# Late modulation on VectorE, query tiles inside the expert stage, and one stage for the even layer's gating and compression

## The reference

```python
mod = silu(c) @ ada_w + ada_b
shift1, scale1, gate1, shift2, scale2, gate2 = jnp.split(mod, 6, axis=-1)
h = rms_norm(x, norm1_g) * (1.0 + scale1) + shift1
z = h @ w_in
att = dilated_mixture_attention(qa, ka, va); rw = rwkv7_bidirectional(...)
x = x + gate1 * (concat([att, rw]) @ w_out)
h2 = rms_norm(x, norm2_g) * (1.0 + scale2) + shift2
q = h2 @ w_query                       # 8 heads of 2 x 128
s1, s2 = q[..., :half] @ sub_keys1.T, q[..., half:] @ sub_keys2.T
# top 16 of each, top 16 of their 256 sums: 16 of 16384 experts per head
ff = sum over 128 experts of gate * gelu(h2 . u_e) * v_e
x = x + gate2 * ff
```

## Time and profile before

| | us |
|---|---|
| median of 3 executions | 2421.84 |
| the profiled execution | 2421.19 |
| its span | 2418.1 |
| TensorE / VectorE / ScalarE / GpSimd busy | 2016.3 / 1547.4 / 1012.2 / 458.9 |
| opening | 0 to 39.5 |
| input projection | 39.5 to 118.6 |
| shift, attention, feature stage | 118.6 to 198.4 |
| recurrence features | 198.4 to 291.9 |
| query projection, scoring | 478.2 to 549.2 |
| experts | 549.2 to 1216.3 |
| swiglu, then norm | 1216.3 to 1428.6 |
| even projection, gating, compression | 1428.6 to 1550.3 |
| last norm, store | 2401.1 to 2418.1 |

### The profile page before, as it was taken

How to read it: one execution, slowest core, us unless ns; L and a number is a source line. 1 busy time by engine, 2 the same in 40 slices (tenths; PEclk the granted TensorE clock), 3 DMA queues, 4 the chain that set the end, 5 groups by cost and what they waited for, 6 DMA issues and landing times. The chain is left out here.

```text
span 2418.1 us, 33750 instructions
## 1 busy us (share of the span) xinstructions
PE 2016.3 (83%) x12086; PEld 1510.8 (62%) x12086; DVE 1547.4 (64%) x2670; ACT 1012.2 (42%) x2036; POOL 458.9 (19%) x475
## 2 busy tenths in 40 slices
PE   4988899695777777778789977899998998648997
PEld 4867888572222232222279976657997987437996
DVE  6577244657767667666456655366676776776665
ACT  3433011333444344444355544156665554315553
POOL 0010023004444443444200000001121433320000
PEclk9965599888999999999999988599999999769999
DMA  7533300237999999999845533114554554204552
GB/s 289 171 100 103 119 3 3 87 124 304 420 419 420 420 420 420 419 420 418 365 139 184 190 123 130 41 39 142 187 191 148 189 181 158 83 35 149 190 184 84
DMA packets 104092, 496.57 MB, mean 205 GB/s; under 512 B 11792, under 2 KB 17040, under 8 KB 71088
## 3 DMA queue, kind: packets, MB, share of 16 engines
q1 hardware_dynamic: 65376, 224.42, 27.8%
q0 software_dynamic: 36864, 268.45, 26.8%
q10 hardware_dynamic: 1744, 2.29, 0.3%
HBM read 494.07 MB, written 1.05 MB: 205 GB/s over the span
## 5 line engine op out<-in xcount | busy, mean ns | idle before, releaser
L239 PE MATMUL ps<-srcs,wh 128*128 128x512 f32 x2064 | 746.8, 403 | 49.1 <-DVE srcs L253 31.0
L1602 PE MATMUL ps<-row,diag 128*128 128x512 f32 x1024 | 507.4, 626 | 155.8 <-ACT diag L1641 155.7
L241 PE MATMUL ps<-srcs,wl 128*128 128x256 f32 x2064 | 586.5, 284 | 0.0
L221 DVE TENSOR_TENSOR wl<-ring,wh 128x1024 fp32r<-128x1024 f32 x362 | 450.2, 1248 | 130.2 <-ACT wh L215 128.6
L239 PEld LDWEIGHTS ps<-srcs,wh 128*128 128x128 f32 x2064 | 395.6, 192 | 144.7 <-issue 40.6
L1602 PEld LDWEIGHTS ps<-row,diag 128*128 128x128 f32 x1024 | 180.0, 193 | 481.8 <-ACT diag L1641 338.5
L1722 DVE CUSTOM_DVE_ANT_0 row<-row,h_tok 128x1024 f32<-128x1024 f32 x256 | 313.7, 1225 | 210.9 <-DMA row<-in_peer_uv,experts 209.1
L215 ACT ACTIVATE wh<-ring 128x1024 fp32r<-128x1024 f32 x362 | 379.5, 1052 | 120.7 <-DMA ring<-in_stream 56.1
L241 PEld LDWEIGHTS ps<-srcs,wl 128*128 128x128 f32 x2064 | 398.9, 193 | 0.1
L1585 POOL DMA_INDIRECT row<-in_peer_uv,experts x256 | 267.4, 1045 | 375.9 <-PE ps L1602 354.4
L231 PE MATMUL ps<-hidh,wh 128*128 128x256 f32 x704 | 199.3, 283 | 9.0 <-DVE hidl L716 6.2
(11 more groups left out here) (449 smaller groups left out, 2319.7 us busy)
## 6 DMA issues: line engine op xcount, KB each, us to landing
ring<-in_stream SPq DMA_DIRECT2D x410, 512.0 KB, 3.3
row<-in_peer_uv,experts POOLq DMA_INDIRECT x256, 15.4
bias<-in_attn_bias SPq DMA_DIRECT2D x8, 256.0 KB, 4.1
w<-in_cmp_w SPq DMA_DIRECT2D x1, 2048.0 KB, 7.2
xT<-in_xT ACTq DMA_DIRECT2D x1, 1024.0 KB, 25.5
out_xT<-hT SPq DMA_DIRECT2D x1, 1024.0 KB, 4.4
lora<-in_lora_up SPq DMA_DIRECT2D x1, 512.0 KB, 3.8
ws<-in_gm_w SPq DMA_DIRECT2D x1, 512.0 KB, 3.4
```

Source lines behind the costliest of these rows:

```text
L221: nc.vector.tensor_tensor(wl[:, n % PAIRS, :], ring[:, tile % RING, :], wh[:, n % PAIRS, :].bitcast(F32), ALU.subtract).then_inc(tiles_fre ...
L239: nc.tensor.matmul(out, wh[:, n, cols], source.rearrange("p a t -> p (a t)"), start=start, stop=stop, skip_group_check=True)
L241: return nc.tensor.matmul(out[:, 0:S], wl[:, n, cols], source[:, 0, :], start=False, stop=stop, skip_group_check=True)
L1602: last = nc.tensor.matmul(y_part(t, half), diag[:, s % DIAGS, :], row[:, s % ROWS, D + half * 512:D + (half + 1) * 512], start=(slot == 0) ...
```

## The change

- The opening loads `xT` on SP's queue behind the first six tiles, takes the mean square ahead of the first column on TensorE, and scales it between two of the last sums on VectorE.
- The 32 late modulation tiles leave the stream. SP loads them from `ada_late` into six slots that lie in `alpha`, `beta`, `kappa`; VectorE adds them up (`late_add`), 20 in the input projection, one per tile, and 12 in the feature stage; TensorE makes 32 columns of the four sums (`late_column`) in the places of the old products. Per stage there is one addition to `mod`. The input projection now also prepares the next projection's first two tiles.
- The query projection and the scoring move into the expert stage: four heads' tiles (8) at its start, interleaved with the choice of heads 0 and 1, the other 8 tiles among the first four heads' slots. Scores are copied by ScalarE instead of VectorE.
- Two swiglus compute the squares and `rstd` at their end; the norm's product goes into the even projection and into the last stage, which stores in four parts from two queues.
- Gating and compression are one stage; its 12 tables are loaded during the projection, ahead of its refills on SP; the compression matmuls alternate between the two halves.

The core of the diff (indentation cut by eight, lines that only move left out):

```diff
     def _(sp):
         for i in range(RING):
             sp.dma_start(ring[:, i, :], A["stream"][i]).then_inc(loaded[i], 16)
+        sp.dma_start(xT[:, :, :], A["xT"].rearrange("(k p) t -> p k t", p=P)).then_inc(x_in, 16)
-        act.dma_start(xT[:, :, :], A["xT"].rearrange("(k p) t -> p k t", p=P)).then_inc(x_in, 16)
...
         dve.wait_ge(c_ready, 1)
         for i in range(T_ADA):
             total, k, slot = acc[:, i // KT, :], i % KT, i % RING
+            if i == T_ADA - 3:
+                dve.wait_ge(summed, 1)
+                nc.vector.tensor_scalar(rstd[:, :], ps[:, 7, 0:S], 1.0 / D, NORM_EPS, ALU.mult, ALU.add
+                                        ).then_inc(scaled, 1)
...
-        take_rstd(dve, summed, scaled, root, inverted)
-        for n in range(AHEAD):
-            low(dve, T_ADA + n)
+        dve.wait_ge(root, 1)
+        nc.vector.reciprocal(rstd[:, :], rstd[:, :]).then_inc(inverted, 1)
+        low(dve, T_ADA)
         dve.wait_ge(columns, 1)
         nc.vector.tensor_tensor(mod[:, 0:T_ADA], ps[:, 0, 0:T_ADA], vec_all("ada_b")[:, 0:T_ADA], ALU.add
                                 ).then_inc(v, 1)
         dve.wait_ge(v, 1)
         nc.vector.scalar_tensor_tensor(gs[:, 0, :], mod[:, 8:16], 1.0, vec_all("norm1_g"), ALU.add, ALU.mult)
+        low(dve, T_ADA + 1)
...
         pe.wait_ge(mats_in, 16)
+        mean_square(pe, squared, summed)
         column(0)
-        mean_square(pe, squared, summed)
         column(1).then_inc(columns, 1)
-def late_load(sp, chunk, count=1):
-    refill(sp, LATE + (chunk - 2) * KT, count * KT)
-def late_tile(pe, chunk, k, begins, counted=None):
-    tile = LATE + (chunk - 2) * KT + k
-    pe.wait_ge(loaded[tile % RING], 16 * (tile // RING + 1))
+late_in = [sem(f"late_in{i}") for i in range(LATE_RING)]
+late_used = sem("late_used")
+def late_load(sp, i):
+    if i >= LATE_RING:
+        sp.wait_ge(late_used, i - LATE_RING + 1)
+    sp.dma_start(late_slot(i), A["ada_late"][i]).then_inc(late_in[i % LATE_RING], 16)
+def late_add(dve, i):
+    k, slot = i % KT, i % LATE_RING
+    total = late_sum(i // KT)
+    dve.wait_ge(late_in[slot], 16 * (i // LATE_RING + 1))
+    if k == 0:
+        last = nc.vector.tensor_scalar(total, late_slot(i), cs[:, k:k + 1], None, ALU.mult)
+    else:
+        dve.wait_ge(late_used, i)
+        last = nc.vector.scalar_tensor_tensor(total, late_slot(i), cs[:, k:k + 1], total, ALU.mult,
+                                              ALU.add)
+    last.then_inc(late_used, 1)
+def late_column(pe, u):
+    pe.wait_ge(late_used, KT * (u + 1))
     for j in range(KT):
+        last = nc.tensor.matmul(ps[:, 7, u * KT + j:u * KT + j + 1], late_sum(u)[:, j * P:(j + 1) * P],
+                                mat("ones")[:, 0:1], start=True, stop=True)
+    return last
...
         @block.sync
         def _(sp):
-            refill(sp, first, total)
+            if loads:
+                loads(sp)
+            if late_count:
+                for i in range(total):
+                    refill(sp, first + i, 1)
+                    if i < late_count:
+                        late_load(sp, i)
+            else:
+                refill(sp, first, total)
...
             for i in range(tok_count):
                 low(dve, first + AHEAD + i)
+                if i < late_count:
+                    late_add(dve, i)
...
-        norm=(lambda k: gs[:, 0, k:k + 1], lambda k: mod[:, k:k + 1]), ahead=False)
-take(T_ADA_LATE)
+        norm=(lambda k: gs[:, 0, k:k + 1], lambda k: mod[:, k:k + 1]), late_count=LATE_W_IN)
...
             nc.tensor.matmul(ps[:, b, :], mat("blockones"),
                              sq[:, 2 * b:2 * b + 2, :].rearrange("p a t -> p (a t)"),
                              start=True, stop=True).then_inc(summed, 1)
-        for k in range(KT):
-            late_tile(pe, 2, k, k == 0)
+        late_column(pe, 0)
+        late_column(pe, 1).then_inc(late_summed, 1)
...
-        late_mod(dve, 2)
+        dve.wait_ge(late_summed, 1)
+        nc.vector.tensor_tensor(mod[:, 16:32], ps[:, 7, 0:16], vec_all("ada_b")[:, 16:32], ALU.add)
...
     def _(sp):
         sp.dma_start(lora[:, :, :], A["lora_up"]).then_inc(ups_in, 16)
         sp.dma_start(g_up[:, :], A["g_up"]).then_inc(ups_in, 16)
+        for i in range(LATE_W_IN + LATE_RING, ADA_LATE):
+            late_load(sp, i)
...
         nc.vector.tensor_tensor(sq[:, 0:4, :], kk[:, :, :], kk[:, :, :], ALU.mult)
+        for i in range(LATE_W_IN, ADA_LATE):
+            late_add(dve, i)
...
-    def _(sp):
-        late_load(sp, 3, 3)
...
-        for chunk in (3, 4, 5):
-            for k in range(KT):
-                late_tile(pe, chunk, k, chunk == 3 and k == 0)
+        late_column(pe, 2)
+        late_column(pe, 3).then_inc(late_summed, 1)
         pe.wait_ge(kb_ready, 1)
...
-        for n in range(AHEAD):
-            high(act, LATE + T_ADA_LATE + n)
...
-        late_mod(dve, 3, 3).then_inc(mod_in, 1)
+        dve.wait_ge(late_summed, 1)
+        nc.vector.tensor_tensor(mod[:, 32:48], ps[:, 7, 16:32], vec_all("ada_b")[:, 32:48], ALU.add
+                                ).then_inc(mod_in, 1)
         dve.wait_ge(mod_in, 1)
         nc.vector.scalar_tensor_tensor(gs[:, 1, :], mod[:, 32:40], 1.0, vec_all("norm2_g"), ALU.add, ALU.mult)
-        for n in range(AHEAD):
-            low(dve, LATE + T_ADA_LATE + n)
...
+        def query(i):
+            pe.wait_ge(tiles_freed, first + i + 1)
+            if i >= 2:
+                pe.wait_ge(query_out, i - 1)
+            for k in range(KT):
+                if i == 0:
+                    pe.wait_ge(src_low, k + 1)
+                last = product_both(query_bank(i), first + i, k, srcs[:, k], k == 0, k == KT - 1)
+            last.then_inc(tiles_used, 1)
...
+        def score(h):
+            pe.wait_ge(query_out, 2 * h + 2)
+            for t in range(TT):
+                for half in range(2):
+                    last = nc.tensor.matmul(score_bank(h)[:, (2 * t + half) * NE:(2 * t + half + 1) * NE],
+                                            queries[:, (2 * h + half) % 4, t * P:(t + 1) * P],
+                                            subkeys[:, half, :], start=True, stop=True)
+            last.then_inc(scored, 1)
...
+        query(0)
+        query(1)
+        pe.wait_ge(keys_in, 16)
+        score(0)
+        turn_h()
+        for h in range(1, EARLY):
+            query(2 * h)
+            query(2 * h + 1)
+            if h >= 2:
+                score(h - 1)
+        score(EARLY - 1)
...
             last.then_inc(v_used, 1)
+            ahead = s // TOPK + EARLY
+            if ahead < NH:
+                if s % TOPK == 3:
+                    query(2 * ahead)
+                if s % TOPK == 8:
+                    query(2 * ahead + 1)
+                if s % TOPK == 13:
+                    score(ahead)
...
+        def copy_low(i):
+            act.wait_ge(tiles_used, split_no(first + i) + 1)
+            nc.scalar.activation(low_part[:, i % 2, :], query_bank(i)[:, S:2 * S], ACT.Copy
+                                 ).then_inc(low_copied, 1)
...
+        for k in range(KT):
+            act.wait_ge(normed, k + 1)
+            nc.scalar.activation(srch[:, k, :], hT[:, k, :], ACT.Copy).then_inc(src_high, 1)
+        weight_and_copy(0)
+        weight_and_copy(1)
+        copy_scores(0)
+        for t in range(TT):
+            act.wait_ge(h_turned, t + 1)
+            nc.scalar.activation(h_tok[:, t, :], ps[:, 2 * t:2 * t + 2, :].rearrange("p b n -> p (b n)"),
+                                 ACT.Copy).then_inc(h_copied, 1)
+        for h in range(1, EARLY):
+            weight_and_copy(2 * h)
+            weight_and_copy(2 * h + 1)
+            if h >= 2:
+                copy_scores(h - 1)
+        copy_scores(EARLY - 1)
...
+            ahead = s // TOPK + EARLY
+            if ahead < NH:
+                if s % TOPK == 5:
+                    weight_and_copy(2 * ahead)
+                if s % TOPK == 10:
+                    weight_and_copy(2 * ahead + 1)
+                if s % TOPK == 15:
+                    copy_scores(ahead)
...
+            if head < NH:
+                dve.wait_ge(score_copied, 2 * head + 2)
...
+        def weight(i):
+            low(dve, first + AHEAD + i)
+        def out(i):
+            dve.wait_ge(low_copied, i + 1)
+            if i >= 4:
+                dve.wait_ge(scored, i // 2 - 1)
+            nc.vector.tensor_tensor(queries[:, i % 4, :], query_bank(i)[:, 0:S], low_part[:, i % 2, :], ALU.add
+                                    ).then_inc(query_out, 1)
...
+        weight(0)
+        out(0)
+        weight(1)
+        out(1)
+        def early_tile():
+            if early() % 4 == 0:
+                at = early.now // 4 + 3
+                if at < 4 * EARLY:
+                    (out if at % 2 else weight)(at // 2)
         for head in range(LOOKAHEAD):
-            choose(head, lambda: None)
+            choose(head, early_tile)
...
+                ahead = head + EARLY
```

(44 more changed lines are left out.)

396 lines of the change are left out of this document (203 added, 193 removed).

## The result

The change takes the median from 2419.5 us (2412.9 to 2422.5, 4 runs) to **2301.4 us** (2296.9 to 2304.4, 4 runs): ratio 0.951, 95% interval 0.949 to 0.954. The profiled execution took 2296.9 us, its span 2295.1 instead of 2418.1, 123.0 us less.

A forecast was written before the change was run, and what follows sets the result against it. The prediction took no engine to bound the whole kernel, each stretch having its own limit. Its terms summed to -121.5 us from the profiled 2421.2, giving 2300 us, with a range of 2285 to 2319.

The forecast's parts named there:

- rival of late tiles: Input projection: late tiles landing in 6.6 us set the pace, 20 steps +9.5, feature stage +2, 2311 us in all; 12%.
- Opening, -1.5: Opening: x lands sooner and the mean square is taken earlier, so the modulation ends at 37.8 us; 1.5 us less.
- Recurrence features, -45: Recurrence's features: the 42.76 us wait behind TensorE's narrow records and two low parts (2.35) go; stage 47 to 49 us.
- features, +3.2: Feature stage: twelve late sums on VectorE take 15.7 us where it idled 12.48; the end moves from 198.3 to 201.5.
- Query projection and scoring, -34.9: Expert stage: gathers start 47 us earlier, less 11.2 for ring loads among them and 0.9 for late row recycling.
- The rival of gathers held up by TensorE in the first four heads: Expert stage: TensorE falls behind in the first four heads, at half clock for 25 us; +13, 2313 us; 8%.
- The rival of a choice that waits: Expert stage: head 0's experts come only after all eight early query tiles; +9, 2309 us; 4%.
- Gating and compression, -36.4: Gating and compression: two stages become one, the 9.7 us table wait goes, paired records take 13.2 instead of 26.3 us.
- the pairing: Compression: records alternating between array halves run in pairs; the rival that they do not overlap costs +13, 2313 us; 5%.
- Norms, -4.7 and -3.7: Even layer's norm: earlier squares -2.4, rstd product moved into the projection -2.3; final norm: squares -2.4, output in four parts -1.3.
- Input projection, +1.5: Input projection: a late sum of 1.28 us in each of 20 steps just fits the 2.84 us period; bank waits cost 1.5.
- Shift and attention, 0: Shift and attention stages: VectorE's chain still ends the shift stage, six late tiles load while transfers idle; no change.

The follow-up runs named there:

- e5: The changed kernel with 192 unused narrow matmuls put back on TensorE's queue ahead of the bonus sums in the recurrence's features; 2344.8 us.
- e6: The changed kernel with the last six ring tiles loaded in the expert stage bringing only 128 of their 1024 columns; 2292.5 us.
- e10: The changed kernel with VectorE taking all eight early query tiles first and choosing the experts of heads 0 and 1 only then; 2306.0 us.
- e1: The changed kernel with one loop order undone: compression matmuls run on one half of the array, then on the other, as before the change; 2309.0 us.
- e4: The changed kernel with each late tile's load issued three steps earlier on SP's queue, five periods before use instead of two; 2296.5 us.
- e8: The changed kernel with 26 unused matmuls added behind the late columns in the stage of shift and norm; 2301.2 us.

## Why the prediction was right

The forecast of 2300 us (measured 2301.4) came out mostly by its own steps, and no rival happened as a whole; of the rival of late tiles the landing did, not the price.

- *Opening, -1.5*: -1.0 from release to release (-2.1 by the marks). The modulation ended at 37.3 us, as forecast (37.8), but one of the two low parts stands behind it now and ends at 38.5.
- *Recurrence features, -45, and features, +3.2*: -45.1 and +3.2. The stage takes 48.4 us from release to release, inside the 47 to 49 that were to show it. e5 shows the cause that I gave.
- *Query projection and scoring, -34.9*: -34.2. The first gather was forecast 32 to 34 us after the stage's first norm operation and came 31.7 after it; nine ring loads fell behind it, as counted, and e6 shows their price. The rival of gathers held up by TensorE in the first four heads did not occur (413 to 419 GB/s from 487 to 640 us). The rival of a choice that waits, built in e10, costs 7.7 us of stage against the +9 that I gave it.
- *Gating and compression, -36.4*: -38.5. Records in pairs took 11.5 us against 13.2: at half clock a pair came every 0.106 us, as forecast (0.103), but the first 96 of the 256 records ran at full clock, a pair every 0.058. e1 prices the pairing at 11.8 against 13.
- *Norms, -4.7 and -3.7*: -6.8 and -5.7, both 2 too small. The sum counted the squares and the products brought forward; from the last updates to TensorE's first record 5.9 us went, of which it has 4.7. In both cases one barrier fewer is passed, which no term had; that this is the rest is argued, not tested.
- *Input projection, +1.5*: +1.9 from release to release (+3.1 by the marks, which count 1.2 us of the opening here), +2.6 in the mean of nine profiles. The size is near by luck. The 1.5 stood for TensorE waiting on VectorE's added work, and that costs 0.2 (e4). The step that failed is that a late tile's two periods before use are enough, taken with the 3.3 us of one load alone: with two in flight the median landing was 5.5 us, the longest 7.0, and that costs 1.7 to 2.4. The rival had this landing (up to 6.6) but made it the length of a period, which is why its +9.5 is four times too much: the next loads are already under way while one lands, and VectorE waited at 8 of 20 tiles.
- *Shift and attention, 0*: +2.1, all in the attention, whose code and inputs are unchanged. It took 30.0 to 34.6 us in kernels that do not differ there, with the mean clock between 0.77 and 0.65; before, 30.1. This is scatter from execution to execution, which goes with how long TensorE stays at half clock (e8).

The errors (opening +0.5, input projection +0.4, attention +2.1, queries +0.7 and the other stages +1 one way, -2.1, -2.1 and -2.0 the other) nearly cancelled: the total is better than the terms, and that part is luck.

On the rule of the Trainium skill (DMA: Bandwidth & Descriptors, Bandwidth) of about 358 GB/s from HBM: over its whole input projection the changed kernel moved 298 GB/s, which cannot tell. The expert stage moved 420 for hundreds of us. The same section measures 425 GB/s for 16 MB with the neighbouring core idle and gives about 358 as a core's share when both stream; this kernel runs on one core, and its 420 agrees with the former. The measurement decides against 358 here.

## What to carry to other kernels

Look for long runs of narrow matmuls on TensorE's queue ahead of something that another engine waits for: their issue cost 0.21 us a record here at half clock, however little they compute, and a vector engine with idle gaps can do the same as weighted sums. In a stage bound by transfers, write down first transfer + bytes behind it / rate + the pause until the first buffer is free; moving the first transfer forward alone gains nothing if it leaves more bytes behind it or uses the buffers up. Issue a tile that a busy engine will need by the slowest landing with as many loads in flight as there will be (7.0 us here), not by the median of a load alone (3.3). And before a stage's length is compared, look at what still runs at its mark: here 1.2 us of the opening looked like a loss of the next stage.
